# Two blocks of a decoder layer joined, the last tile's transposes set among the first gate/up products, and two weight splits moved ahead

## The reference

```python
mix = jnp.concatenate([hm, ha, hs], axis=-1) @ w_out          # 1024 x 1024
x = x + rms_norm(mix, norm_w[1])
h = rms_norm(x, norm_w[2])
ff = (jax.nn.silu(h @ w_gate) * (h @ w_up)) @ w_down          # 1024 -> 2816 -> 1024
return x + rms_norm(ff, norm_w[3])
```

## Time and profile before

| | |
|---|---|
| median of 3 runs | 2979.31 us |
| profiled execution, its own time | 2981.53 us |
| its span, first to last instruction | 2979.7 us |
| mean granted TensorE clock | 0.971 of full speed |
| PE busy | 2826.2 us (95%) |
| PE weight loads, beside its matmuls | 2271.7 us (76%) |
| DVE / ACT / POOL busy | 1230.3 / 925.9 / 900.5 us |
| gate/up matmuls (L2047), 4224 | 1653.6 us busy |
| down matmuls (L2061), 2112 | 829.1 us busy |

### The profile page before, as it was taken

One profiled execution on the slowest core, in us unless ns is written; L12 is line 12 of the kernel. 1 busy time (PEld: TensorE's weight loads), 2 busy tenths in 40 slices (PEclk: granted clock), 3 DMA queues, 4 the chain that ended last, 5 costly groups with the idle time before them and its releaser, 6 DMA issues. The chain is left out here.

```text
span 2979.7 us, 34350 instructions
## 1 busy us (share of the span) xinstructions
PE 2826.2 (95%) x13396; PEld 2271.7 (76%) x13396; DVE 1230.3 (41%) x2170; ACT 925.9 (31%) x1619; POOL 900.5 (30%) x450
## 2 busy tenths in 40 slices
PE   6999999998999999999769999999989999999997
PEld 5678877777788888888656788777777888888885
DVE  4479854764011221111435798547630112211114
ACT  4337334663111111111233364347521111111112
POOL 1238310430233322223313383104202323222333
PEclk9999999899999999999979999999999999999998
DMA  4113310622111111111341133106121111111113
GB/s 127 43 29 92 114 52 17 179 73 90 38 50 57 42 56 42 42 49 49 113 129 29 29 92 113 52 18 193 64 85 36 50 56 56 42 42 49 42 49 127
DMA packets 233982, 201.90 MB, mean 68 GB/s; under 512 B 20480, under 2 KB 209024, under 8 KB 233744
## 3 DMA queue, kind: packets, MB, share of 16 engines
q1 hardware_dynamic: 228112, 179.45, 19.9%
q10 hardware_dynamic: 5760, 20.97, 1.8%
HBM read 161.60 MB, written 38.80 MB: 67 GB/s over the span
## 5 line engine op out<-in xcount | busy, mean ns | idle before, releaser
L2047 PE MATMUL ps<-act_hi,whi 128*128 128x512 f32 x1408 | 551.6, 392 | 19.8 <-POOL wlo L1954 14.5
L2047 PE MATMUL ps<-act_lo,whi 128*128 128x512 f32 x1408 | 551.1, 391 | 0.0
L2047 PE MATMUL ps<-act_hi,wlo 128*128 128x512 f32 x1408 | 550.9, 391 | 0.0
L2081 DVE TENSOR_TENSOR hf<-sg,ps 128x1024 f32<-128x1024 f32 x44 | 53.7, 1221 | 931.1 <-PE ps L2047 931.1
L785 PE MATMUL ps<-act_hi,whi 128*128 128x512 f32 x960 | 394.3, 411 | 9.0 <-ACT smr L540 8.4
L785 PE MATMUL ps<-act_lo,whi 128*128 128x512 f32 x960 | 377.9, 394 | 0.0
L785 PE MATMUL ps<-act_hi,wlo 128*128 128x512 f32 x960 | 377.9, 394 | 0.0
L1954 POOL TENSOR_TENSOR wlo<-raw,whi 128x1024 fp32r<-128x1024 f32 x84 | 200.2, 2395 | 499.1 <-ACT whi L1991 499.1
L1201 DVE TENSOR_SCALAR_CACHE_REDUCE ties<-score,kth 128x384 uint8<-128x384 f32 (+5 forms) x396 | 348.4, 943 | 4.8
L2047 PEld LDWEIGHTS ps<-act_hi,whi 128*128 128x128 f32 x1408 | 266.4, 189 | 77.1 <-issue 21.4
L2087 DVE TENSOR_TENSOR yacc<-yacc,ps 128x1024 f32<-128x1024 f32 x176 | 214.8, 1220 | 264.6 <-PE ps L2061 264.6
(11 more groups left out here) (287 smaller groups left out, 3906.1 us busy)
## 6 DMA issues: line engine op xcount, KB each, us to landing
raw<-in_w_in SPq DMA_DIRECT2D x56, 512.0 KB, 3.8
raw<-in_w_up SPq DMA_DIRECT2D x44, 512.0 KB, 3.9
raw<-in_w_gate SPq DMA_DIRECT2D x44, 512.0 KB, 3.8
raw<-in_w_down SPq DMA_DIRECT2D x44, 512.0 KB, 3.5
proj_scratch<-stage ACTq DMA_DIRECT2D x40, 512.0 KB, 2.7
wc<-proj_scratch SPq DMA_DIRECT2D x14, 1280.0 KB, 6.7
xmid_scratch<-xres SPq DMA_DIRECT2D x16, 512.0 KB, 2.6
wo_raw<-in_w_out SPq DMA_DIRECT2D x10, 512.0 KB, 7.5
```

The source lines that it names most:

```text
L2047: mm = pe.matmul(ps[:, 2 * s + half, :], w[:, k], a[:, k, cols], start=(k == 0 and m == 0), stop=(k == KT - 1 and m == 2))
L2081: v.tensor_tensor(hf[:, :], sg[:, :], unit_psum(1), ALU.mult).then_inc(hidden.sem, 1)
```

## The change

Blocks B and E of a layer become one block without a barrier between them (the stages are now functions, and `together(mix, feed)` runs one after the other on each engine). Waits on semaphores take the place of the barrier: POOL waits for the last transpose before it clears `yacc`, SP for the last `d_mix` before it loads the last norm's weights, ACT for the stores of `xres` before group 1.

On PE, the first two runs of `gate_up(0)` are issued as four halves: gate half 0 in front of the last tile's transposes, then the transposes, then up half 0, gate half 1, up half 1. Only the last two need the last tile's `act_lo`.

ACT and POOL split the first unit of group 1 at the end of group 0, ahead of the split of group 0's last product (groups 1 and 2 are written out now, the loop starts at 3). The two units of the last `down` are split into `whi`/`wlo`, which are free once the last `gate_up` has ended (wait on `pj`), instead of `dhi`/`dlo` (wait on `y_ps`).

The diff without the lines that only change their indentation:

```diff
 # block B, PE
-                    turn(NT - 1)
+                    turn_normed(pe, t - 1)          # turn(NT-1) is now in E
 # block E, SP
                     gate_up(0, U_FF)
+                sp.wait_ge(*d_mix(L, NT))
                     sp.dma_start(nrow[0][:, :], ...)
 # block E, POOL
                     def body(b, p, u):
-                        if not isinstance(b, int):
-                            ring_lo(u, 0, wlo, whi)
-                            ring_lo(u + 1, 1, wlo, whi)
+                    first = isinstance(b, int) and b == 0
+                    if not first:
+                        if not (isinstance(b, int) and b == 1):
+                            ring_lo(u, 0, wlo, whi)
+                        ring_lo(u + 1, 1, wlo, whi)
                         ring_lo(u + 2, 0, wlo, whi)
                         hid_lo(b, 0, p)
                         ring_lo(u + 3, 1, wlo, whi)
-                        if not (isinstance(b, int) and b == 0):
+                    if first:
+                        ring_lo(u + 4, 0, wlo, whi)
+                    else:
                             ring_lo(u + 4, 0, dlo, dhi)
                             ring_lo(u + 5, 1, dlo, dhi)
                         hid_lo(b, 1, p)
+                pool.wait_ge(*d_turn(L, NT))
                     ...
-                    body(0, 0, U_FF)
-                    with pool.Fori(0, FB // 2) as i:
+                for b in range(3):
+                    body(b, b % 2, U_FF + max(6 * b - 2, 0))
+                with pool.Fori(1, FB // 2) as i:
                     ...
-                        ring_lo(N_UNITS - 2 + j, j, dlo, dhi)
+                    ring_lo(N_UNITS - 2 + j, j, wlo, whi)
 # block E, ACT: body changed in the same way (ring_hi(u + 4, 0, whi) before hid_hi(0, 1))
                     body(0, 0, U_FF)
+                for s in range(2):
+                    act.wait_ge(*x_out[s](L, 16 * NT // 2))
                     ...
-                    act.wait_ge(*y_ps(L, NT * (FB - 1)))
+                act.wait_ge(*pj(L, 4 * FB))
                     for j in range(2):
-                        ring_hi(N_UNITS - 2 + j, j, dhi)
+                    ring_hi(N_UNITS - 2 + j, j, whi)
 # block E, PE
+                pe.wait_ge(*w_lo(L, U_FF + 1))
+                pe.wait_ge(*d_lo(L, NT // 2))
+                pe.wait_ge(*d_mix(L, NT - 1))
+                half_unit(0, 0)
+                turn_normed(pe, NT - 1)
+                pe.wait_ge(*w_lo(L, U_FF + 2))
+                pe.wait_ge(*d_mix(L, NT))
+                half_unit(1, 0)
+                pe.wait_ge(*d_lo(L, NT))
+                half_unit(0, 1)
+                half_unit(1, 1)
                     gate_up(0, U_FF)                # now only j = 1
                     ...
-                            down(b - 1, p, u + 4)
-                    down(FB - 1, 0, N_UNITS - 2)
+                        down(b - 1, p, u + 4, dhi, dlo)
+                down(FB - 1, 0, N_UNITS - 2, whi, wlo)
```

More of the change, by code:

```diff
@@ new lines, in a_scalar @@
+                    else:
+                        whole(u)
+                    extras(u - 1)
+                    if U_XBC <= u - 1 < U_XBC + 8:
+                        conv_silu(u - 1)
+                    if U_XBC <= u < U_XBC + 8:
+                        conv_taps(u)
+                    if u >= U_SZ:
+                        act.wait_ge(*evicted(u))
+                        spill_unit(u)
+                for k in range(N_PAIRS, N_PAIRS + 4):
+                    attend(k)
+                hi_rows(NT - 1)
@@ L2034, in _ @@
                 @block.tensor
                 def _(pe):
-                    def gate_up(b, u):
-                        for j in range(2):
-                            for s in range(2):
-                                pe.wait_ge(*w_lo(L, u + 2 * j + s + 1))
-                                if not (isinstance(b, int) and b == 0 and j == 0):
-                                    pe.wait_ge(*(silu if s == 0 else hidden)(L, 2 * b + j))
-                                wh, wl = tiles(whi[s][:, :]), tiles(wlo[s][:, :])
-                                for half in range(2):
-                                    cols = slice(half * HALF, (half + 1) * HALF)
-                                    for k in range(KT):
-                                        for m, (w, a) in enumerate(((wh, act_hi), (wh, act_lo), (wl, act_hi))):
-                                            mm = pe.matmul(ps[:, 2 * s + half, :], w[:, k], a[:, k, cols],
-                                                           start=(k == 0 and m == 0), stop=(k == KT - 1 and m == 2))
-                                mm.then_inc(pj.sem, 1)
@@ L2051, in down @@
-                    def down(b, p, u):
-                        pe.wait_ge(*w_lo(L, u + 2))
-                        pe.wait_ge(*h_lo(L, 2 * b + 2))
-                        for t in range(NT):
-                            pe.wait_ge(*y_add(L, NT * b + t + 1))
-                            rows = slice(t * P, (t + 1) * P)
-                            for half in range(2):
-                                cols = slice(half * HALF, (half + 1) * HALF)
-                                for j in range(2):
-                                    for m, (h, w) in enumerate(((hhi, dhi), (hhi, dlo), (hlo, dhi))):
-                                        mm = pe.matmul(ps[:, 4 + 2 * (t % 2) + half, :], h[p][:, j, rows], w[j][:, cols],
-                                                       start=(j == 0 and m == 0), stop=(j == 1 and m == 2))
-                            mm.then_inc(y_ps.sem, 1)
@@ L2100, in _ @@
[L2100 to L2107 removed]
+                    for _, _, _, _, vector in stages:
+                        vector(v)
@@ L2111 @@
+        stages = [layer(L) for L in range(DEPTH)]
+        for project, mix, feed in stages:
+            together(project)
+            together(mix, feed)
 _INS = ["x", "positions", "norm_w", "w_in", "mlstm_gate_bias", "mlstm_norm_w", "conv_w", "conv_b", "dt_bias", "a_log",
```

2829 lines of the change are left out of this document (1426 added, 1403 removed).

## The result

The changed kernel takes 2927.65 us (median of 4 runs, 2924.3 to 2930.16) against 2979.97 us (4 runs, 2976.0 to 2981.78) for the kernel before: ratio 0.9825, 95% interval 0.9808 to 0.9843. Forecast were 2921.3 us, with a range of 2915 to 2932. The profiled execution took 2928.78 us, its span is 2926.9 us, the mean granted clock 0.977 (0.971 before).

A forecast was written before the change was run, and what follows sets the result against it. PE, busy for 95% of the span, was taken as the bound. Savings of 10.6 + 9.87 + 8.52 = 28.99 us a layer, 58.0 for two, gave 2921.3 us; own range 2917 to 2925, overall 2915 to 2932.

The forecast's parts named there:

- place A: Where block B meets E: gate half 0 covers PE's wait for normed tile 7; 10.6 us a layer saved.
- first rival: The clock falls all the same where block B meets E: 3.2 to 5.2 us in all; chance 0.08.
- Place B: From group 0 to group 1: PE's 7.25 us wait and 2.62 us of low clock go; 9.87 us a layer.
- The unseen cost: PE's loop entry from group 0 to 1, so far inside the 7.25 us wait; taken as 0, at most 7.1.
- second rival: PE's loop entry shows between groups 0 and 1: 0.3 to 9.7 us a layer; chance 0.07.
- Place C: The last down: its units are split beside `down(9)`, so PE's wait before `down(10)` goes; 8.52 us a layer.
- Third: Rival: one of the 1.0 and 3.7 us margins is not there; 11.2 us, giving 2932.5; chance 0.04.
- fourth rival: One of the three moves fails through a late semaphore: 2938.3 without the smallest, 2979.3 without all; chance 0.03.
- The margins: Slack before PE needs the splits: 1.0 us for unit 32 in group 0, 3.7 us for unit 35 in group 1.
- Fifth rival: Block E's loop settles behind the weight splits, making it slower: 2996 us at 16 us of delay; chance 0.02.
- the baseline: Whole kernel: the profiled execution's 2981.53 us, taken as 2.2 us above the median, turns 2923.5 into 2921.3.
- PE's busy time: Sign in the profile after: PE's busy time falls by some 7 us a layer, its idle time by 21.

The follow-up runs named there:

- e6: Changed kernel with the last tile's transposes again in front of every gate/up product, blocks still joined: 2940.63 us, ratio 0.9866.
- e7: Changed kernel with gate half 1 directly behind the last tile's transposes, ahead of up half 0: 2931.01 us, ratio 0.9839.
- e2: Kernel before with only the last down's units split into whi/wlo: 2968.31 us, ratio 0.9947.
- e4: Kernel before with only blocks B and E joined and the last tile's transposes among the first gate/up halves: 2957.84 us, ratio 0.9932.
- e1: Changed kernel run again, unaltered: 2927.49 us, ratio 0.9825.
- e9: Changed kernel run once more, unaltered, beside the repeat of e8: 2924.28 us, ratio 0.981.
- e3: Kernel before with only group 1's first unit split ahead of group 0's product, groups 1 and 2 written out: 2962.89 us, ratio 0.9941.
- e8: Changed kernel with the first two of up half 0's eight contraction steps also ahead of the last tile's transposes: 2921.01 us, ratio 0.9793.
- e10: Repeat of e8, the changed kernel with two contraction steps more ahead of the transposes: 2921.36 us, ratio 0.98.
- e12: Changed kernel with both e8's two steps ahead of the transposes and e11's added products in the scans: 2922.36 us, ratio 0.9794.
- e11: Changed kernel with eight added products, overwritten unread, in front of one chunk's transposes in each layer's scans: 2928.69 us, ratio 0.9822.

## Why the prediction was right, and where it was off

**The range.** 2927.65 us lies in the stated range of 2915 to 2932, but above the 2917 to 2925 that the prediction gives as the forecast's own. The range reached that far because of rivals (the clock at place A, PE's entry into its loop, a margin), and none of them came. That the whole time is inside is therefore in part luck; what holds by its mechanism is the saving at the three places.

**Place A.** Forecast 10.6 us a layer, measured 10.8 and 10.5. The step holds in its parts: 0.87 us of wait are left, transposes of 1.09 us, then no stop. That barrier and branch were inside this sum is shown by e6. The clock did not fall there (first rival): 10 times out of 10, two in each of the five profiled executions that have this place as the changed kernel has it, at 18.89 to 18.91 us. The Trainium skill, page "TensorE: Matmul & The Clock Gate", section "Part 4: PE-mode transpose", says that a transpose doesn't count as busy time of PE in the same way. These ten can't tell, since the clock stayed up with or without them; e7, where the clock falls only after a further 2.37 us, doesn't contradict it either.

**Place B.** Forecast 9.87, measured 10.1 and 9.9. The unseen cost, PE's entry into its loop, is nothing that the trace can show: the 360 matmuls across it take 81.64 us, and 360 x 0.2269 = 81.68. The second rival is out. The rule of the Trainium skill, page "Runtime: NRT & Kernel Launch", section "Instruction fetch mechanics", that a taken branch to code that isn't resident stops the engine, names a cost which doesn't appear here; whether the code was resident no row tells.

**Place C.** Forecast 8.52, measured 8.45 and 8.38: 2.87 us from add to add and not 2.73. From the first add of `down(10)` to the end it is 35.1 us, and as much before; the tail kept its pace, as assumed.

**Third and fourth rival.** The margins were 0.9 and 3.6 us, forecast 1.0 and 3.7, and each of the three parts alone takes away its own wait and no other (e2 to e4).

**Fifth rival.** The loop did not settle behind the splits: from the third `hf` to the last it takes 610.18 us in layer 1 before and after, and 610.09 in layer 2 before and after.

**The sum.** By the traces 58.2 us, forecast 58.0; by the medians 52.3. The step that is off is the baseline, "it was 2.2 us above the median, so the forecast is 2921.3": it took the untouched 1450 us as the same in the two medians. They aren't to within some us, since the clock in the scans and the time of block A come out differently from run to run. The mean of before over 57 runs is 2981.7 us, 2.4 above the median I started from; with it the traces' saving gives 2923.5, and the changed kernel's mean over 14 runs is 2926.7. That leaves 3.2 us (95% interval some +-2.1), 2.6 of it in the untouched part, which comes to 1450.3 us in the one and 1452.9 in the other by these means. PE's busy time says that the difference between executions is clock and not waits. Forecast were some 7 us less a layer; by the prediction's own terms it should have been 29.0 - 21.2 = 7.8, 15.6 in all. In the profiled execution it is 2826.2 - 2817.5 = 8.7, and in e1 2826.2 - 2808.8 = 17.4. Against the runs of before beside each group the changed kernel's mean is 52.0, 52.8 (e1) and 57.7 us (e9) less, so the last group has next to nothing of the loss. Why the untouched part should be longer in the changed kernel is open. The 0.9 us of idle time at place A isn't it by e4, which has that place and whose untouched part is 1449.5 us by the mean of its 6 runs, like those of e2, e3, e7, e8, e10 and e12 (1449.2 to 1450.5); high beside the changed kernel are e6 (1452.4, 4 runs) and e11 (1455.1, 5 runs). It may be chance, for which e9 speaks and the lengths of the low clock in layer 2 speak against; no run here settles it.

## What to carry to other kernels

Where PE is the bound, list its waits, and price each as its own length plus what the matmuls behind it lose at the low clock; each of the three places came out within 0.3 us a layer here. A wait at a joint is covered best with work that needs nothing from the late tile, and there must be some of it on both sides of the tile's transposes (e7 against the changed kernel: 4.2 us a layer for the order of two halves). Before measuring a gain of under 1%, find the stretch that varies by itself and take means over enough runs of both kernels; cut at landmarks, one trace of each gave the gain at the places as 58.2 us, where medians of 4 runs gave 52.3 for the whole.

## What the runs showed of the hardware

Idle times of 2.3 to 2.4 us for `catr` in sparse work are where the clock falls in the scans: at 27 of the 29 such waits of all traces, where the wait of 1.25 us later in the scans brought none in 28. How long it stays low differs between two executions of one kernel at the same wait (worked out from the rows' mean clocks, some 13.7 us after the change against 3.4 in e1). A long fall also slows PE enough that its next wait disappears. A filled wait brings that next wait back, and with it the fall in three of four cases (e11 and e12); in layer 1 of e11 the clock stayed at 1.00. At place A, between long runs, 0.87 us of idle time and 1.09 us of transposes never brought it down.

DVE's scaling in the tail takes longer once POOL adds the residual beside it; that POOL is the cause isn't shown by an experiment. Timeline of DVE and of POOL after the change:

```profile
2895.69 1.28 DVE L2117 SCALAR_TENSOR_TENSOR yacc<-yacc,small,nrow 128x1024 f32<-128x1024 f32 x1
...
2901.59 2.52 DVE L2117 SCALAR_TENSOR_TENSOR yacc<-yacc,small,nrow 128x1024 f32<-128x1024 f32 x1
```

```profile
2897.04 2.41 POOL L1978 TENSOR_TENSOR resid<-resid,yacc 128x1024 f32<-128x1024 f32 x1 [20.40 <-DVE yacc L2117]
```

The first, before POOL starts, takes 1.28 us, the third 2.52, while DVE's adds from PSUM stay at 1.21 to 1.22. It is so before the change too, so it costs nothing in the comparison. DVE has no idle time between the second scaling and the last, and POOL idles 1.16 us ahead of each addition, so these scalings set the tail's pace.
